# Latent attention, VectorE's order: the odd head's probabilities scaled on both sides of the next queries, the copy of the even head's turned ones behind both

## The reference

```python
q = (rms_norm(q_lat, g) @ w_uq).reshape(B, S, 8, 96)
q_nope, q_rope = q[..., :64], rope(q[..., 64:], pos)
s = einsum('bqhc,bkc->bhqk', q_abs, ckv) + einsum('bqhr,bkr->bhqk', q_rope, kr)
p = softmax(where(mask, s * MLA_SCALE, -inf), axis=-1)
lat = einsum('bhqk,bkc->bqhc', p, ckv)
y_mla = einsum('bshc,chv->bshv', lat, w_uv)
```

## Time and profile before

| | |
|---|---|
| time without profile | 2734.69 us, median of 3 (2734.59 to 2735.32) |
| profiled execution | 2736.36 us, span 2734.5 us, mean granted TensorE clock 0.999 |
| TensorE busy | 2707.9 us, 99% (21622 matmuls) |
| VectorE busy | 1793.7 us, 66% |
| ScalarE busy | 1180.0 us, 43% |
| GpSimd busy | 528.0 us, 19% (216 subtractions of weights on L506) |
| DMA | 257.93 MB, mean 94 GB/s |

### The profile page before, as it was taken

The page is one execution under the profiler, slowest core; times in us unless marked ns, Lnnn a source line. Parts: engine busy times, 40 slices in busy tenths (PEclk is TensorE's granted clock), DMA queues, the critical chain, the costliest instruction groups (busy, mean ns, idle before and its releaser), DMA issues.

```text
span 2734.5 us, 53707 instructions
## 1 busy us (share of the span) xinstructions
PE 2707.9 (99%) x21622; PEld 2633.2 (96%) x21622; DVE 1793.7 (66%) x2810; ACT 1180.0 (43%) x1842; POOL 528.0 (19%) x220
## 2 busy tenths in 40 slices
PE   8999999999999999999999999999999999999998
PEld 8999999799999999999999999987999999999998
DVE  6777765656436578777687776566554365777775
ACT  4343454522345463433454334544224464634344
POOL 0000024234372310000300001331443723100002
PEclk9999999999999999999999999999999999999999
DMA  4333323132362122233333333221223621233332
GB/s 156 99 102 94 96 74 96 35 93 88 93 216 80 53 86 93 94 101 93 89 94 94 100 93 94 87 88 35 90 87 93 216 77 55 86 93 93 93 101 72
DMA packets 75770, 257.93 MB, mean 94 GB/s; under 512 B 10704, under 2 KB 15696, under 8 KB 74256
## 3 DMA queue, kind: packets, MB, share of 16 engines
q1 hardware_dynamic: 68432, 240.66, 28.5%
q10 hardware_dynamic: 7104, 13.94, 1.4%
HBM read 246.70 MB, written 7.87 MB: 93 GB/s over the span
## 4 chain that ended last, share of the span: by engine, by line
PE 95%; DVE 2%; ACT 1%; DVEq 1%; issue 1%; ACTq 0%; DMA 0%; PEldq 0%
PE PS L516 94%; PE PS L929 0%; DVE O L1854 0%; ACT LNT L1319 0%; DVEq L2373 0%; DVE P L2381 0%; ACTq L1627 0%; DVEq L2581 0%; ACT P L1319 0%; DVE SC L2361 0%; DMA WR<-in_w 0%; ACT WH L1319 0%; PE PS L1254 0%; ACT Y L1319 0%; DVE BL L1851 0%
## 5 line engine op out<-in xcount | busy, mean ns | idle before, releaser
L506 POOL TENSOR_TENSOR WL<-WR,WH 128x1024 fp32r<-128x1024 f32 x216 | 527.8, 2456 | 2167.6 <-ACT WH L1319 2167.6
L516 PE MATMUL PS<-XH,WH 128*128 128x272 f32 x2464 | 595.2, 291 | 7.5 <-DVE XL L1851 7.5
L516 PE MATMUL PS<-XL,WH 128*128 128x272 f32 x2464 | 588.1, 289 | 0.0
L1319 ACT ACTIVATE WH<-WR 128x1024 fp32r<-128x1024 f32 x450 | 464.0, 1051 | 189.3 <-DMA WR<-in_w 158.6
L516 PEld LDWEIGHTS PS<-XH,WH 128*128 128x128 f32 x2464 | 425.6, 189 | 11.5 <-issue 8.2
L516 PE MATMUL PS<-XH,WL 128*128 128x272 f32 x2464 | 426.8, 288 | 0.2 <-DVE WL L1851 0.2
L516 PEld LDWEIGHTS PS<-XL,WH 128*128 128x128 f32 x2464 | 426.2, 189 | 0.3
L1319 ACT ACTIVATE LNT<-PS 128x272 f32<-128x272 f32 (+5 forms) x350 | 154.0, 450 | 578.2 <-PE PS L516 562.7
L516 PEld LDWEIGHTS PS<-XH,WL 128*128 128x128 f32 x2464 | 354.2, 188 | 0.7 <-DVE WL L1851 0.4
L516 PE MATMUL PS<-HH,WH 128*128 128x272 f32 x1408 | 298.4, 289 | 0.0
L516 PE MATMUL PS<-HL,WH 128*128 128x272 f32 x1408 | 297.3, 288 | 0.0
(11 more groups left out here) (284 smaller groups left out, 5014.3 us busy)
## 6 DMA issues: line engine op xcount, KB each, us to landing
WR<-in_w SPq DMA_DIRECT2D x450, 512.0 KB, 3.6
MRAW<-in_mem ACTq DMA_DIRECT2D x2, 1024.0 KB, 4.9
MKs<-in_memk_in ACTq DMA_DIRECT2D x2, 1024.0 KB, 6.7
MVs<-in_memv_in ACTq DMA_DIRECT2D x2, 1024.0 KB, 10.0
out_mem_k<-MKp ACTq DMA_DIRECT2D x2, 1024.0 KB, 5.7
out_mem_v<-MVp ACTq DMA_DIRECT2D x2, 1024.0 KB, 8.2
out_y<-Y SPq DMA_DIRECT2D x3, 544.0 KB, 3.0
Y<-in_x ACTq DMA_DIRECT2D x2, 544.0 KB, 6.6
```

The costliest lines, as they stand in the source:

```text
L506: pool.tensor_tensor(WL[s][:, :], WR[s][:, :], WH[s][:, :].bitcast(F32), ALU.subtract).then_inc(lo_ready[s], 1)
L516: return pe.matmul(out, lhsT, rhs, start=start, stop=stop, skip_group_check=True)
L1319: return act.activation(out, in_, func, **kw)
```

## The change

Only the order of VectorE's program in the four passes changes: part 0 of the odd head is scaled ahead of the even head's next queries, and part 1 behind them, and the copy of the even head's turned probabilities, which stood first, stands behind both. No instruction is added or taken away, and no semaphore, buffer or other engine's order is changed.

```diff
                 for p in range(4):
                     a, b = 2 * p, 2 * p + 1
                     maxima(b, 1)
-                    pt_copy(a)
+                    normalize(b, 0)
                     if p < 3:
                         queries(a + 2)
-                    normalize(b, 0)
                     normalize(b, 1)
+                    pt_copy(a)
                     if p < 3:
                         queries(b + 2)
                     pt_copy(b)
```

## The result

The changed kernel takes 2744.43 us (median of 7 runs) where the kernel before takes 2735.04 (median of 7): a ratio of 1.0037, 95% interval 1.0027 to 1.0047, or **9.4 us slower**. The prediction was 2739.7, +0.18%, with 2741.5 as its upper end. The direction held and the size did not: the loss is nearly twice the 5.0 us that were worked out, and outside the range.

The account below looks back on a forecast made before the run. TensorE, holding 95% of the chain, was taken as the bound. Four passes of +1.26 us, with 0 for p=0 and p=3, gave +5.0 us: 2741.4 profiled, shifted by 1.67 to 2739.7 us (+0.18%), range 2733.0 to 2741.5.

Parts of the forecast that it names:

- the 2.2 us idle: p=1, 2: TensorE's odd queries wait for the held even-query multiplication, idling 2.2 us where it was 0.15.
- rival 3: TensorE's rate falls after the idle: 27 matmuls 0.1 us slower each, 2.7 us a pass, 2750.5 us; chance 0.06.
- The meeting and the hold: p=1, 2: part 0's scalings meet GpSimd's subtraction, holding the even-query multiplication; next scores +1.26 us in each of four passes.
- Who comes first: p=1, 2: VectorE's 128x384 scaling starts 0.05 us before GpSimd's subtraction and goes through; the 128x128 scaling stands.
- rival 1: GpSimd gets in first despite the 0.05 us: 0.12 us more a pass, 2740.2 us; chance 0.72 together with the forecast.
- p=0: No GpSimd meeting; later multiplication against saved 0.25 us idle: 0 taken, ends of -0.2 and +0.3 us each.
- p=3: No queries there; part 1's reciprocal still waits for ScalarE's exponentials and ends the chain: 0.
- The copy's move: Copy of the even head's turned probabilities behind part 1's scalings: costs nothing, ending before the next scores.
- Rival 2: VectorE keeps access over both part 0 scalings, GpSimd starts behind: 0.37 us less a pass, 2733.2; both forms 0.15.
- No contact at all: Rival 2's second form, engines never meeting: scores 0.88 us earlier a pass, 2731.2 us; both forms' chance 0.15.
- The rule of exclusive access: Two-port VectorE instructions and GpSimd lock each other out for a whole instruction, first issuer winning; same sum, +5.0 us.

Follow-up runs that it names:

- two filled kernels: Changed kernel, TensorE computing the second half of the even head's next queries three times or twice in p=1, 2: 2740.3 and 2739.69 us.
- the kernel that comes nearest to it: Changed kernel, GpSimd's subtraction in p=1, 2 waiting for VectorE's scaling of the odd head's part 0: 2734.97 us, ratio 1.0001.
- with the meeting taken away: Changed kernel, ScalarE's conversion of a weights chunk in p=1, 2 moved between its two copies of turned probabilities: 2732.07 us, ratio 0.9988.
- the conversion's move: Kernel before, ScalarE's conversion in p=1, 2 moved from ahead of the odd head's exponentials to between two copies: 2733.9 us, ratio 0.9995.
- the kernel with the idle made: Changed kernel, GpSimd's subtraction behind part 1, plus waits and three drained copies on VectorE ahead of the queries in p=1, 2: 2745.49 us, ratio 1.0037.

## Why the prediction was wrong

**What failed is one step: TensorE's clock behind the idle was left out of the sum.** The prediction worked the 2.2 us idle out rightly and then took the 27 matmuls behind it at full speed. It named the fall as rival 3 but gave it 0.06, "TensorE is busy on both sides of the idle" being the argument against. The trace of before held no idle of that length, so nothing in it could speak for full speed; that absence was read as evidence. The Trainium skill, page "TensorE: Matmul & The Clock Gate", section "Why this matters for your kernels", warns of gaps over about 3 us. That figure would not have counted this idle. Here idles of 2.19 to 2.50 us brought the fall in 10 of 12 passes, so the measurement decides against that figure.

**Rival 3's price was also off**, by half: 2.7 us a pass against 1.4. It assumed 0.1 us on each of 27 matmuls, which takes a half rate of over 5 us. Each of the ten falls lasts 3.4 us, and by my estimate from that, half of a stretch of 3.4 us, it can't cost over 1.7. In the changed kernel ten of the twelve odd queries still start at the full rate; half rate meets the last two and the transposes (2.33 instead of 1.27), and is over 0.14 us into the scores. In the one pass whose clock is at half from the first odd query on, the cost is 10.19 - 8.66 = 1.53. With the 1.4 and 1.5 now measured, in three passes, the sum would have read 5.0 + 4.3 = 9.3 us.

The other steps:

- **The meeting and the hold**: right in kind and size. 1.26 a pass was forecast; 8.38 to 8.43 less 7.23 gives 1.15 to 1.20. The idle was to be 2.2 and is 2.19 to 2.22. The four passes of before are less alike than the prediction has them: the 128x384 scaling took 751 ns in p=1 of layer 0, and 892 to 906 in the other three, where it starts 0.13 to 0.15 us earlier in the pass and ends at the same point. That fits a scaling that stands until GpSimd is nearly done.
- **Who comes first**: VectorE by 0.05 us was forecast and GpSimd came first, in all four passes (rival 1). That is the profiled execution with the clock of 0.946, where GpSimd starts 2.17 us into the pass. In the two filled kernels it starts at 2.23 as in the kernel before, and VectorE is first by 0.05 to 0.06 us in all eight passes, as forecast; which came first in the changed kernel's other executions is not on record. Rival 1's price of 0.12 a pass did not appear: 8.43 with GpSimd first, 8.38 to 8.42 with VectorE first. The order of the tie decides which scaling stands, 2581 or 2419 ns, and not when both are done.
- **p=0**: nothing in layer 0 (6.76, as before; 0.52 us idle ahead of the odd queries, none ahead of the transposes). In layer 1 it costs 0.28, near the upper end given (+0.3). It varies with the execution: the other kernels with the new order in p=0 and the copy behind it have 6.62 to 6.84 in layer 0 and 6.66 to 7.07 in layer 1. In the changed kernel's layer 1 part 0's reciprocal waits 0.45 us for ScalarE's exponentials, and both multiplications now stand behind it. VectorE's timeline:

```profile
1844.35 0.45 DVE L2364 TENSOR_SCALAR SC<-SC 128x3 f32<-128x3 f32 x1
1845.24 0.17 DVE L2372 RECIPROCAL SC<-SC 128x2 f32<-128x2 f32 x1 [0.45 <-ACTq L1627]
1845.49 0.61 DVE L2381 TENSOR_SCALAR P<-P,SC 128x384 f32<-128x384 f32 x2
```

- **p=3**: 0, as said (6.38 and 6.03 against 6.38 and 6.01).
- **The copy's move**: free, shown by the kernel that makes it alone.
- **Rival 2's price**: 0.37 shorter was worked out, 0.15 measured in the kernel that comes nearest to it. The difference is GpSimd's start, 0.23 us later behind the semaphore than rival 2 has it; with that put in, the sum gives 0.14. A GpSimd instruction that waits through both scalings, as rival 2 has it, was seen in no run: in the filled kernels it got in between them.
- **No contact at all**: 0.88 shorter was worked out; with the meeting taken away three passes are 0.96 to 0.97 shorter (6.26) and p=1 of layer 0 is 0.68 shorter (6.55). Of the 0.97, 0.48 are what the conversion's move gives the old order too.
- **The rule of exclusive access** (the Trainium skill, page "SBUF — State Buffer", section "Who interferes with whom": whoever issues first has the shared ports for the whole instruction) agrees with the rows of scalings shown here, though at 498.73 in the changed kernel the two starts are the same to 0.01 us and who was first shows only in the lengths. The rows near 2179 us, which the prediction counts with it, are subtractions of two operands in SBUF and no scalings, so they show the exclusion for another kind of instruction. The runs add one thing: a GpSimd instruction that waits gets in between two VectorE scalings that would otherwise overlap by 0.08 us.

What stays open: why two passes of twelve keep their clock. In the changed kernel the idle of p=1 of layer 1 is 2.20 us, the same as that of p=1 of layer 0, and the matmuls around it are the same; in the kernel with the idle made, p=1 of layer 1 keeps the full clock behind 2.48 us. So the length of the idle alone does not decide, and the place of the fall varies too, from the restart itself to 1.5 us behind it. No run here tells a length at which the fall begins: idles of 1.41 to 1.44 us had none in four passes, and nothing between these and 2.19 was tried.

## What to carry to other kernels

Before moving a VectorE scaling from SBUF to SBUF, look at what GpSimd runs at its new place: the same move costs 1.2 us a pass at the start of a 2.4 us GpSimd instruction and gains 0.5 where there is none. Count an idle of over 2 us ahead of TensorE twice, for itself and for the half rate that may follow (1.3 to 1.5 us here). Matmuls that only repeat a result can fill it: 6 or 12 of them were enough here. And where two starts are tied, move the neighbour (here one line of ScalarE's order) rather than reckon the tie.

## What was not expected of the hardware

- Behind idles of 2.19 to 2.50 us the granted clock fell to the 1.2 GHz level in 10 of 12 passes. The fall came between the restart itself and 1.5 us behind it (1.0 to 1.2 us in the changed kernel), and lasted 3.4 us each time (503.10 to 506.51 in the stretches above). Behind idles of 0.70 to 0.72 and 1.41 to 1.44 us it did not fall, in eight passes.
- It cost 1.3 to 1.5 us a pass: ten transposes of 128 columns took 2.33 us instead of 1.27, and matmuls of 272 columns were spaced 0.22 us instead of 0.125.
- A VectorE multiplication that reads PSUM is not held by GpSimd (0.84 us for two under a subtraction, as without one), while a scaling as small as 32x160 is (1.16 us instead of 0.29).
